# One step in four of the experts' weighted row sum moves from VectorE to TensorE

## The reference

```
a = gelu(einsum('nhkd,nd->nhk', u[ek], xk))
y = einsum('nhk,nhkd->nd', gk * a, v[ek])
x = layer_norm(ALPHA * x + y)
```

## Time and profile before

| | |
|---|---|
| median of 3 executions | 2763.49 us (2759.49 to 2781.48) |
| profiled execution, span | 2750.8 us |
| median minus that span | 12.7 us |
| TensorE matmul busy | 2018.4 us, 73% of the span |
| VectorE busy | 1539.8 us, 56% |
| ScalarE busy | 415.0 us, 15% |
| GpSimd busy | 692.8 us, 25% |
| gathers (software queue) | 608.21 MB, 56.5% of the 16 DMA engines |
| mean granted TensorE clock | 0.828 of full speed |

### The profile page before, as it was taken

The page is one execution under the profiler, slowest core; times in us unless marked ns, Lnnn a source line. Parts: engine busy times, 40 slices in busy tenths (PEclk is TensorE's granted clock), DMA queues, the critical chain, the costliest instruction groups (busy, mean ns, idle before and its releaser), DMA issues. The chain is left out here.

```text
span 2750.8 us, 21320 instructions
## 1 busy us (share of the span) xinstructions
PE 2018.4 (73%) x6651; PEld 989.5 (36%) x6651; DVE 1539.8 (56%) x3816; ACT 415.0 (15%) x1168; POOL 692.8 (25%) x612
## 2 busy tenths in 40 slices
PE   8956688895666867779786766776867767666766
PEld 3544446372122233334452332531223344222222
DVE  0063431377987453433559366488377647966665
ACT  0000231001111011111111122111123111111111
POOL 4000000002232222222232132233133424244542
PEclk9975565997888987778788988898988889888888
DMA  8201001437688897777887989997988999699997
GB/s 277 78 1 21 14 1 53 162 123 298 227 329 308 332 353 275 286 291 278 292 311 276 348 311 364 361 360 270 399 328 338 409 392 368 244 407 421 422 419 296
DMA packets 190137, 759.36 MB, mean 276 GB/s; under 512 B 22204, under 2 KB 79432, under 8 KB 116168
## 3 DMA queue, kind: packets, MB, share of 16 engines
q0 software_dynamic: 84480, 608.21, 56.5%
q1 hardware_dynamic: 105544, 149.80, 15.9%
HBM read 752.35 MB, written 5.60 MB: 276 GB/s over the span
## 5 line engine op out<-in xcount | busy, mean ns | idle before, releaser
L1750 PE MATMUL ps<-uv,diag 128*128 128x512 f32 (+1 forms) x1884 | 1059.4, 705 | 373.0 <-ACT diag L1726 339.7
L1638 POOL DMA_INDIRECT uv<-in_experts_dram,slots x576 | 662.2, 1150 | 1993.9 <-PE ps L1750 1332.6
L1658 DVE CUSTOM_DVE_ANT_0 uv<-uv,x 128x1024 f32<-128x1024 f32 x512 | 622.9, 1223 | 305.6 <-DMA uv<-in_experts_dram,slots 176.0
L1750 PEld LDWEIGHTS ps<-uv,diag 128*128 128x128 f32 (+1 forms) x1884 | 368.9, 210 | 940.3 <-ACT diag L1726 453.7
L1726 ACT ACTIVATE diag<-const,wgt 128x128 f32<-128x128 f32 (+1 forms) x471 | 164.2, 385 | 810.6 <-DVE wgt L1668 779.6
L1713 ACT ACTIVATE gelu<-dot 128x2 f32<-128x2 f32 x288 | 58.6, 203 | 673.7 <-DVE dot L1658 668.3
L1680 DVE SCALAR_TENSOR_TENSOR acc<-uv,wgt,acc 128x1024 f32<-128x1024 f32 x100 | 128.1, 1281 | 0.0
L421 PE MATMUL ps<-even_w,xT 128*128 128x512 f32 (+3 forms) x240 | 96.9, 559 | 0.9 <-DMA even_w<-in_even_w_in_dram 0.9
L1658 DVE CUSTOM_DVE_ANT_0 uv<-uv,xs 128x1024 f32<-128x1024 f32 x64 | 78.3, 1226 | 29.1 <-DMA ffn_gb<-in_ln_ffn_b_dram 14.0
L704 PE MATMUL ps<-sample_s_kTs,sample_s_q_b 64*32 64x256 f32 x256 | 62.2, 414 | 43.9 <-DVEq L1782 43.9
L421 PEld LDWEIGHTS ps<-even_w,xT 128*128 128x128 f32 (+1 forms) x240 | 37.5, 163 | 59.9 <-issue 56.1
(11 more groups left out here) (414 smaller groups left out, 2109.5 us busy)
## 6 DMA issues: line engine op xcount, KB each, us to landing
uv<-in_peer_w_q_dram SPq DMA_DIRECT2D x16, 1024.0 KB, 11.9
sample_cache<-in_cache_dil_kv_dram SPq DMA_DIRECT2D x64, 256.0 KB, 8.6
sample_cache<-in_odd_w_in_dram SPq DMA_DIRECT2D x12, 1024.0 KB, 8.5
first_w<-in_odd_w_in_dram SPq DMA_DIRECT2D x12, 1024.0 KB, 9.6
last_w<-in_odd_w_in_dram SPq DMA_DIRECT2D x12, 1024.0 KB, 13.0
uv<-in_experts_dram,slots POOLq DMA_INDIRECT x576, 8.9
even_w<-in_even_w_in_dram SPq DMA_DIRECT2D x8, 1024.0 KB, 8.6
sample_w<-in_peer_w_q_dram SPq DMA_DIRECT2D x8, 1024.0 KB, 13.9
```

The lines of the kernel that those rows point to most:

```text
L1638: self.k.nc.gpsimd.indirect_dma_start(out=self.uv[:, s % RING, :], out_offset=None, in_=self.table, in_offset=bass.IndirectOffsetOnAxis(ap ...
L1658: ins = nc.vector.tensor_tensor_reduce(self.uv[:, s % RING, 0:D], self.uv[:, s % RING, 0:D], x, 1.0, 0.0, ALU.mult, ALU.add, self.dot[:, g ...
L1750: last = nc.tensor.matmul(k.bank(c)[0:m, :], self.diag[:, s % RING, 0:m], self.uv[:, s % RING, D + 512 * c:D + 512 * (c + 1)], start=(j == ...
```

## The change

The four entries of the table that gave VectorE the steps with `s % 4 == 3` are emptied. `by_dve` is then false for every step, `shared` for every visit.

```diff
@@ -1563,13 +1563,13 @@
 WINDOWS = (
     ("route 0 0", FIRST[0], ()),
     ("route 0 1", FIRST[1], ()),
-    ("mixer 2", FIRST[1] + 30, (3,)),
+    ("mixer 2", FIRST[1] + 30, ()),
     ("route 1 2", FIRST[2] + 16, ()),
-    ("mixer 0", FIRST[2] + 46, (3,)),
+    ("mixer 0", FIRST[2] + 46, ()),
     ("route 1 0", FIRST[3] - 16, ()),
-    ("mixer 1", FIRST[3] + 16, (3,)),
+    ("mixer 1", FIRST[3] + 16, ()),
     ("route 1 1", FIRST[5] - 34, ()),
-    ("nothing", FIRST[5], (3,)),
+    ("nothing", FIRST[5], ()),
 )
```

## The result

| | before | changed |
|---|---|---|
| median of 7 executions | 2763.49 us (2752.98 to 2781.48) | 2800.95 us (2789.03 to 2816.94) |
| profiled execution, span | 2750.8 us | 2788.9 us |
| the same from the first step's dot to the end | 2102.1 us | 2128.7 us |

The changed kernel is slower by a ratio of 1.0123, 95% interval 1.0087 to 1.0158: 24 to 44 us.

What follows compares the result with a forecast made beforehand. The prediction took TensorE's list to bound mixer 2 and the gathers' DMA the last visit; 38 + 15 + 16 + 0 - 9 = +60 us gave 2823.5 us, range 2760 to 2890.

Steps and rivals of the forecast that it cites:

- Mixer 2, forecast +38: In mixer 2, 29 moved steps at 1.72 us lengthen TensorE's list, the longest there; partly hidden, +38 us remain.
- 49.9 - 6.9 - 5: Mixer 2: 49.9 us added to TensorE, less 6.9 hidden in four large gaps and 5 in `diag` waits.
- Folds and end: Four folds vanishing within the stream give -7 us, and a shorter last burst and fold at the end -2: -9.
- Mixer 0, forecast +15: In mixer 0, 17 moved steps add 29.2 us to TensorE, of which waits hide half: +15 us.
- I let them hide half: Mixer 0: waits for `diag` and query weights, 24.5 us, were taken to hide half of the 29.2 us added.
- Mixer 1, forecast +16: Mixer 1 in three parts: 8.6 us count in the first, 7 in the second, nothing in the DMA-bound third.
- What goes from VectorE: 0: The 131.7 us taken from VectorE gain nothing, as it stands idle about half the time in the mixers.
- The last visit, forecast 0: In the last visit 32 more steps on TensorE fit behind the gathers, 2.485 us a step: 0 us.
- The ring's slack: Last visit: some 3.7 us can be lost on TensorE, through the ring of buffers, before the DMA queue runs dry.
- (b): Rival: denser matmuls turn low-clock time into full-clock time, saving 20 us in mixer 2, some 35 in all: 2788; chance 0.10.
- (a): Rival: waits for `diag` or weights in the mixers hide nearly all added work, 2765 to 2775 us; chance 0.17.
- (d): Rival: VectorE's adds delay `diag` in the mixers, so removing them gains 35 us: faster, -35 - 9, 2719; chance 0.08.

Runs made afterwards that it cites:

- e6: Kernel before plus 105 x 2 matmuls on zeros where the change puts moved steps, VectorE's adds and the folds kept; ratio to before 1.0179, mixer 2 582.9 us.
- e3: Kernel before with VectorE's 100 adds replaced by one-element memsets giving the same signal, TensorE's list unchanged; ratio to before 1.0037, mixer 1 376.9 us.
- e4: Changed kernel with VectorE's 105 adds kept as well, into a sum nobody reads, no folds; ratio to before 1.0106, mixer 1 400.7 us.
- e2: Changed kernel with VectorE's 29 adds of mixer 2 put back, all other steps moved; ratio to before 1.0021, mixer 2 555.7 us.
- e5: Changed kernel, but VectorE adds every second step of mixer 2 (57 adds); ratio to before 0.9977, mixer 2 544.6 us.
- e9: Against the kernel before: VectorE adds every second step in mixers 2 and 1, none in the last visit, mixer 0 unchanged; ratio 1.0000, mixer 1 395.0 us.
- e10: Kernel before without its five folds, all adds kept; ratio to before 0.9980, last visit 338.4 us.

## Why the prediction was right, and where it was not

The direction and the range held, and the mechanism: TensorE's list in mixer 2. The size was 60 us against a measured ratio worth 34 (24 to 44); the last visit came out as forecast, and every other term was too large. Over all profiles that share a setting the means are as follows.

- **Mixer 2, forecast +38, measured about +26.** With 29 adds and TensorE as before: 545.1, 549.8, 555.7, 544.4, mean 549. With all steps on TensorE: 568.4, 585.5, 582.9, 563.9, mean 575. With 57 adds: 544.6, 529.2, 539.5, mean 538. The groups overlap only between the first and the third, and e6 ascribes the cost to TensorE's matmuls alone. (e3, 560.5 with the adds emptied, is in no group; it too lies below the second.) The step that was mis-sized is the subtraction "49.9 - 6.9 - 5". In the profile pair the list grew by 39.7 us instead of 49.9, though a moved step's records took 1.83 and not 1.72: 3.6 are the fold, which the forecast had booked under "Folds and end", 3.4 are other matmuls, and 4.6 are overlap of records. The waits gave 16.7 instead of 11.9: 12.2 for `diag`, where I had 5, and 3.1 in the long gaps, where I had 6.9.
- **Mixer 0, forecast +15, measured +1** (277.8 us in the six kernels with 17 adds and TensorE's list of before, 279.0 in the three with none). TensorE's busy time grew by 19.7 us (227.8 - 208.1), not by 29.2, and its idle time took 18.7 of them: `diag` fell from 15.0 to 5.4 us, the query weights from 9.5 to 3.7. The clock rose from 0.88 to 0.93. e6 shows the same with the load alone. The step that failed is "I let them hide half".
- **Mixer 1, forecast +16, measured +6.** Here two terms meet. The four settings, with means of five, one, two and three profiles (first row, then second):

| mixer 1, us | VectorE adds 27 | no adds |
|---|---|---|
| TensorE's list as before | 384.9 | 376.9 |
| all steps on TensorE | 401.7 | 391.3 |

TensorE's part is 14 to 17 us. That it is the forecast's 16 is luck, for the places are wrong. Of the three parts (steps 304 to 325, 326 to 377, and 378 to 413) the forecast lengthened the first by 8.6 us, the second by 7 and the third by nothing. With the adds kept (e4 and e6 against the five profiles of the first row) they grew by 5, 5 and 7; with the adds gone (changed, e2 and e5) by 3, -1 and 5. VectorE's part is -8 to -10, on one profile in the first row, which the forecast put at nothing ("What goes from VectorE: 0"): that step failed here. It was in waits for weights, not for `diag` (e3).

In mixer 0 (275.3 with the adds emptied) and the last visit (339.4) the nothing holds within the scatter; in mixer 2 e3 shows nothing clear of the spread. And it is a matter of stretches alone: the whole executions of e3 and e4 show no gain from leaving the adds out. I had taken hiding from idle shares, and VectorE is idle 42% of mixer 1; the kernel e9, whose 28 more adds made mixer 1 longer by 10 us, says how little that share tells.
- **The last visit, forecast 0: right.** It stayed with the gathers at 421 GB/s. The two bursts in four steps are those foreseen, at the full clock:

```profile
2601.53 3.70 PE L1750 MATMUL ps<-uv,diag 128*128 128x512 f32 x8 [1.27 <-ACT diag L1726]
...
2606.50 3.70 PE L1750 MATMUL ps<-uv,diag 128*128 128x512 f32 x8 [1.26 <-ACT diag L1726]
```

They are 4.97 us apart for two steps, 2.485 each. The cover of the gathers was enough. The ring's slack was not called upon, as the clock stood at 1.00 there.
- **Folds and end, forecast -9, measured about -4 in the last stretch and none elsewhere.** The last visit to the end took 336.1 to 337.1 us in the four kernels with all steps on TensorE and no fold there (changed, e2, e4, e5), mean 336.7, and 339.4 to 341.3 in the five with both folds, mean 340.4. The fold ahead of the last visit's norm is 1.6 of it, the end up to 1.7 (e10). Of the other three folds two stood in mixers, where they are part of what was measured above, and one beside routing, where nothing came back (steps 272 to 304 took 112.8 us instead of 112.9). And the stretch behind mixer 2, steps 176 to 206, took 105.7 to 106.7 us instead of 104.3 to 104.5 in every kernel whose mixer 2 has more or less of the steps' matmuls on TensorE than the kernel before; it was not in the sum, and why is open.
- Together: 26 + 2 + 1 + 6 - 4 = +31, beside the 34 of the ratio.
- **The rivals.** That the clock pays, (b), was part of what happened: the mean clock of mixer 2 rose by 0.04, that of mixer 1 by nearly 0.05 and that of mixer 0 by 0.05, which is the sign that the prediction had set against itself. With the rule of the Trainium skill cited there ("TensorE: Matmul & The Clock Gate", HAM oscillation) the trace agrees: in the last visit, with its gap of 2.83 us in four steps reduced to two of 1.27, the clock went from 0.87 to 1.00. What it was worth in mixer 2 is not 20 us: the other matmuls gained 3.4 in the profile pair, inside the scatter of unchanged kernels (226 to 231 us), and in the last visit it was worth nothing. (a) described mixer 0 alone. (d) had the right sign for VectorE's part, in mixer 1 only, but not the way: emptying the adds took 7 us of all `diag` waits, not 35. Those waits fell because TensorE came later to them: e6, with all adds kept, has 9.0 us of them in mixer 2 where the kernel before has 18.7. ScalarE's 42 us came to 29.7, since the second `diag` of a pair adds 0.29 and not 0.40. For GpSimd no run isolates a gain.

**What stays open.** Mixer 2 differs by up to 11 us between four profiles of one and the same list, and by 22 between those with all steps moved. The granted clock differs with it (0.83 in 585.5 and 582.9 us, 0.85 in 568.4 and 563.9), but whether the clock sets the time or follows the stalls was not tried. What of e3's 560.5 us is such scatter can't be told either.

## What to carry to other kernels

An engine that is idle 20 or 40% of a stretch may still be what the stretch waits for: price a moved operation in each stretch by itself, and look up what ended the idle time, since the same 1.7 us per step lengthened one mixer by half of their sum, another by a third (TensorE's part of mixer 1), and a third mixer and the last visit by next to nothing. Take load from one engine and give it to another only as far as a two-by-two of both loads says (here 8 to 10 us against 14 to 17 in mixer 1), and measure the next portion anew: the next 28 steps, which by these prices should have gained 7 us, cost 10. And profile the unchanged kernel twice before a stretch's difference of 10 us is explained.

## What the runs showed of the hardware

- With 105 more steps' worth of matmuls the mean clock rose in every mixer (0.81 to 0.85, 0.88 to 0.93, 0.88 to 0.92), and it fell when steps were taken away (0.74 to 0.77 in mixer 2 with 57 adds on VectorE). A step's records in mixer 2 took 2.36 to 2.44 us in the mean with 29 adds, 2.25 to 2.30 with none, and 2.73 to 2.76 with 57. The other matmuls there took 226 to 231 us with 29 adds and 223 to 230 with none, which is not clear of the scatter, but 232 to 248 with 57. Thus taking a third of the steps' matmuls off TensorE freed less than their price: its busy time in mixer 2 was 390 to 406 us against 422 to 430.
- Matmuls on a zero stationary operand raised the clock as real ones did (0.94 in mixer 0, where the changed kernel has 0.93).
- A start of a gather on GpSimd took 0.94 us when neither a dot nor an add of VectorE ran in its first 0.9 us (the middle eight tenths of 239 such starts lie between 0.94 and 0.95), and longer when one did: the median is 1.49 us beside an add and 0.96 beside a dot alone, and a tenth of each took over 1.78 (kernel before).
- The part of the program ahead of the first step took 648.7 us in one profile and 654.9 to 660.9 in eleven others of programs that are the same there.
